# 192 instead of 160 of the 576 tokens take their experts by gathered rows, with 64 of them searched in the first tile's parts

## The reference, cut to what matters

```
q = (tb @ w_q).reshape(PEER_BLOCK, PEER_HEADS, 2, PEER_HALF)           # 8 heads, 2 x 128
s = einsum('thik,hink->thin', q, sub_keys)                             # 2 x 128 scores a head
s_top, i_top = top_k(s, 16)
cand = s_top[:, :, 0, :, None] + s_top[:, :, 1, None, :]
best_s, best_c = top_k(cand, 16)                                       # 16 experts of 16384 a head
eid = i1 * N_KEYS + i2;  g = softmax(best_s)
act = gelu(einsum('thkd,td->thk', u_tab[eid], tb))
out = einsum('thkd,thk->td', v_tab[eid], g * act)
```

## Time and profile before

| | us |
|---|---|
| median of 3 runs (lowest, highest) | 2275.99 (2273.0, 2285.11) |
| the profiled execution | 2277.83 |
| its span, first to last instruction | 2276.1 |
| PE busy | 2229.8 (98%) |
| DVE busy | 1585.5 (70%) |
| POOL busy | 1475.2 (65%) |
| ACT busy | 814.1 (36%) |

### The profile page before, as it was taken

One profiled execution on the slowest core, in us unless ns is written; L12 is line 12 of the kernel. 1 busy time (PEld: TensorE's weight loads), 2 busy tenths in 40 slices (PEclk: granted clock), 3 DMA queues, 4 the chain that ended last, 5 costly groups with the idle time before them and its releaser, 6 DMA issues.

```text
span 2276.1 us, 38281 instructions
## 1 busy us (share of the span) xinstructions
PE 2229.8 (98%) x14510; PEld 2152.9 (95%) x14510; DVE 1585.5 (70%) x2800; ACT 814.1 (36%) x1201; POOL 1475.2 (65%) x851
## 2 busy tenths in 40 slices
PE   8999999999999999999999999999989999999998
PEld 8999999997799999999999999999989999999998
DVE  7866444546678336768978889898478777777774
ACT  4443223432133002133433344444344444444442
POOL 5554333432354555557878887889778888888873
PEclk9999999999999999999999999999999999999999
DMA  6224323225763233248888897999999999999982
GB/s 215 84 80 137 97 92 101 93 96 194 250 230 128 84 126 94 84 132 275 304 286 289 291 313 248 300 331 318 355 364 396 374 369 374 385 370 375 381 311 79
DMA packets 212800, 535.19 MB, mean 235 GB/s; under 512 B 16816, under 2 KB 101168, under 8 KB 210224
## 3 DMA queue, kind: packets, MB, share of 16 engines
q1 hardware_dynamic: 111392, 234.65, 31.7%
q0 software_dynamic: 46080, 167.79, 19.7%
q10 hardware_dynamic: 55184, 130.77, 15.7%
HBM read 453.89 MB, written 79.25 MB: 234 GB/s over the span
## 4 chain that ended last, share of the span: by engine, by line
PE 85%; DVE 7%; POOL 2%; DMA 2%; ACT 1%; issue 1%; ACTq 0%; DVEq 0%; SPq 0%; POOLq 0%
PE ps L1008 47%; PE ps L732 30%; PE ps L1066 2%; POOL w_lo L706 1%; DVE prev L1875 1%; PE ps L909 1%; DMA gbuf<-gate_scratch 1%; POOL ug L698 1%; PE ps L896 1%; PE ps L904 1%; PE ps L1021 1%; PE ps L913 1%; PE ps L929 1%; DVE n_lo L1991 1%; DVE oh L2097 1%
## 5 line engine op out<-in xcount | busy, mean ns | idle before, releaser
L673 POOL TENSOR_SCALAR w_hi<-raw 128x1024 fp32r<-128x1024 f32 x129 | 139.5, 1081 | 516.3 <-issue 384.0
L706 POOL TENSOR_TENSOR w_lo<-raw,e_hi 128x1024 fp32r<-128x1024 f32 x128 | 326.4, 2550 | 95.2 <-PE ps L1008 85.3
L706 POOL TENSOR_TENSOR w_lo<-raw,w_hi 128x1024 fp32r<-128x1024 f32 x128 | 318.9, 2492 | 86.6 <-PE ps L1008 84.5
L1008 PE MATMUL ps<-p_hi,w_lo 128*128 128x416 f32 x1024 | 361.4, 353 | 0.0
L1008 PE MATMUL ps<-g_hi,w_lo 128*128 128x416 f32 x1024 | 359.6, 351 | 0.0
L675 POOL TENSOR_TENSOR w_lo<-raw,w_hi 128x1024 fp32r<-128x1024 f32 x129 | 320.7, 2486 | 10.8
L732 PE MATMUL ps<-h_hi,w_hi 128*128 128x288 f32 (+2 forms) x1216 | 273.0, 306 | 1.6 <-ACT ma L1342 1.6
L732 PE MATMUL ps<-h_lo,w_hi 128*128 128x288 f32 (+2 forms) x1216 | 262.1, 297 | 0.0
L732 PE MATMUL ps<-h_hi,w_lo 128*128 128x288 f32 (+2 forms) x1216 | 261.7, 296 | 0.0
L2075 DVE CUSTOM_DVE_ANT_0 ug<-ug,ps 128x1024 f32<-128x1024 f32 x160 | 192.3, 1213 | 72.2 <-DMA ug<-rows_u,eid 56.4
L698 POOL DMA_INDIRECT ug<-rows_u,eid x160 | 214.8, 1342 | 37.5 <-issue 24.3
(11 more groups left out here) (358 smaller groups left out, 5086.0 us busy)
## 6 DMA issues: line engine op xcount, KB each, us to landing
raw<-units SPq DMA_DIRECT2D x385, 512.0 KB
gate_scratch<-gt SPq DMA_DIRECT2D x52, 512.0 KB
activation_scratch<-ge ACTq DMA_DIRECT2D x120, 208.0 KB
abuf<-activation_scratch ACTq DMA_DIRECT2D x30, 832.0 KB
gbuf<-gate_scratch ACTq DMA_DIRECT2D x30, 832.0 KB
prev<-ssm_in ACTq DMA_DIRECT2D x8, 1024.0 KB, 6.7
ssm_s<-prev ACTq DMA_DIRECT2D x8, 1024.0 KB, 4.5
cxb<-parked_tiles ACTq DMA_DIRECT2D x8, 870.0 KB, 6.8
```

The source lines that it names most:

```text
L673: pool.tensor_scalar(w_hi[:, s, :], raw[:, r, :], 1.0, 1.0, ALU.mult, ALU.mult).then_inc(s_whi, 1)
L706: pool.tensor_tensor(w_lo[:, n % 2, :], raw[:, n % RAW, :], e_hi[m % HS_].bitcast(F32), ALU.subtract)\
L1008: last = mm(accp[par], w[:, k * P:(k + 1) * P], x_[:, k, t0:t0 + ND], start=k == 0 and i == 0, stop=k == KT - 1 and i == 2)
```

## The change

`SPREAD` goes from 4 to 2: 64 spread tokens (the columns 384 to 447), each dealt over two partitions. So 192 tokens are gathered, by 192 gathers of each table, and `ND` is 384: three whole tiles and 24 gate blocks. The half tile is gone. In its place each of the four parts of the first tile carries a third "head row" (`SLOTS` = 3): in partitions 0 to 63 one of its two heads, in 64 to 127 the other, of the 64 spread tokens. The part's scores take two PSUM banks instead of one, with four more matmuls. `column_of` finds a row's place in the tables of indices and dots.

The order is written anew: `UT` = [5, 26, 26, 26], so the search ends at unit 83 and 34 units remain beside the 24 blocks; `DOTS_T` = [0, 42, 43, 43], so all 128 dots of the last 128 tokens lie in the three searches. 24 dots of spread tokens go beside the blocks, for which their h rows are turned into PSUM once more (`h_beside`, before block 2); 8 before the last eight U units, two in each of those, two in each of the first eight V units. `M_RING` is 40 instead of 53. `scores_out(j+1)` is done at two thirds of a tile instead of half.

```diff
-SPREAD = 4
+SPREAD = 2
+SLOTS = PAIR + 1
+PART_ROWS, PART_SPREAD = PAIR * TOPK, TOPK
+PART_COLS = SLOTS * TOPK
-TT = [(T_ROWS, PH)] + [(t, PH) for t in range(0, T_HALF, P)] + [(T_HALF, PH // 2)]
-assert T_HALF % P == 0 and T_HALF <= ND
+TT = [T_ROWS] + [t for t in range(0, T_HALF, P)]
+assert T_HALF % P == 0 and T_HALF == ND
-UT = [4, 20, 20, 20, 10]
+UT = [5, 26, 26, 26]
-M_RING = M_TILE[3] + 9
+M_RING = M_TILE[2] + 9
-DOTS_T = [0, 26, 26, 26, 12]
+DOTS_T = [0, 42, 43, 43]
-DOTS_B = [(b + 1) * (N_PICK - N_SEARCH) // NB - b * (N_PICK - N_SEARCH) // NB for b in range(NB)]
-DOTS_U = [9, 0, 0, 1, 1, 1, 1, 1, 1]
-DOTS_V = [2, 2, 2, 2, 2, 2, 3, 2]
+N_BESIDE = 24
+B_SPREAD = 2
+DOTS_B = [0] * B_SPREAD + [(b + 1) * N_BESIDE // (NB - B_SPREAD) - b * N_BESIDE // (NB - B_SPREAD)
+                           for b in range(NB - B_SPREAD)]
+N_TAIL = N_PICK + N_BESIDE
+DOTS_U = [8, 2, 2, 2, 2, 2, 2, 2, 2]
+DOTS_V = [2, 2, 2, 2, 2, 2, 2, 2]
+def column_of(k):
+
+    c, a = divmod(k, PART_ROWS) if k < N_PICK else divmod(k - N_PICK, PART_SPREAD)
+    return c * PART_COLS + a + (PART_ROWS if k >= N_PICK else 0)
...
-    use += [(k, TAIL + (k - N_PICK) * 2 * GI // (N_ROW - N_PICK)) for k in range(N_PICK, N_ROW)]
+    use += [(k, TAIL + (0 if u < 0 else GI // 2 + u // 2 if u < GI else u)) for u in range(-1, 2 * GI) for k in tail_dots(u)]
...
-                for i in range(4 * c, 4 * c + 4):
-                    last = mm(ps[:, 4 + c, i % 4 * P:(i % 4 + 1) * P], q[:, i, T_ROWS:TK], key_sb[:, i, :],
+                if c >= 2:
+                    pe.wait_ge(s_scs, c - 1)
+                to = [part_scores(c)[:, r // SLOTS, r % SLOTS * NKEYS:(r % SLOTS + 1) * NKEYS] for r in range(2 * SLOTS)]
+                for i in range(2 * PAIR):
+                    qi = 2 * PAIR * c + i
+                    mm(to[i], q[:, qi, T_ROWS:TK], key_sb[:, qi, :], start=True, stop=True)
+                for i in range(2 * PAIR):
+                    qi = 2 * PAIR * c + i
+                    p0 = i // 2 * HALF
+                    last = mm(to[2 * PAIR + i % 2][p0:p0 + HALF], q[:, qi, T_HALF:T_HALF + HALF], key_sb[:, qi, :],
                               start=True, stop=True)
...
                 gates(b, b % 2, b == 0)
+                if b == B_SPREAD - 1:
+                    pe.wait_ge(s_ud, N_PICK)
+                    turn_rows(1, spread_columns, h_beside)
...
-                    if m == m0 + (n // 2 + 2 if j else n - 1) and j + 1 < len(TT):
+                    if m == m0 + (2 * n // 3 + 1 if j else n - 1) and j + 1 < len(TT):
                         scores_out(j + 1)
-                    if j and m == m0 + 3 * n // 4 + 1:
+                    if j and m == m0 + 7 * n // 8 + 1:
...
-                    act.wait_ge(s_ud, N_PICK)
+                    act.wait_ge(s_ud, N_TAIL)
...
             for c in range(PARTS):
-                search(c + 1, c * PAIR, PAIR, lambda cols: None)
+                search(c + 1, part_rows(c), SLOTS, lambda cols: None, last_of_tile=c == PARTS - 1)
...
+            dve.wait_ge(s_sc, PARTS - 1 + len(TT))
+            spread_cols = (a[:, :, ND:T_ROWS].bitcast(F32).unsqueeze(2).to_broadcast([P, KT, SPREAD, NX])
+                           for a in (g_hi, g_lo))
+            tt_(g_spread[:], *spread_cols, ALU.add).then_inc(s_gp, 1)
             one_hots(0, 0)
             for b in range(NB):
+                if b == B_SPREAD:
+                    dve.wait_ge(s_hr, 2)
                 if b + 1 < NB:
                     one_hots(b + 1, (b + 1) % 2, dots_of(b))
```

More of the change, by code:

```diff
@@ L150, in tail_dots @@
     after = DOTS_U + DOTS_V
-    d0 = N_PICK + sum(after[:u + 1])
+    d0 = N_TAIL + sum(after[:u + 1])
     return range(d0, d0 + after[u + 1])
@@ L421, in trunk, with part_scores, part_rows @@
         acc_spread = h_spread = ps[:, 6:8, :]
+        h_beside = ps[:, 2:4, :]
+        def part_scores(c):
+            return ps[:, 4 + c % 2 * 2:6 + c % 2 * 2, 0:SLOTS * NKEYS]
+        def part_rows(c):
+            return sc[:, c % 2 * PH:c % 2 * PH + 2 * SLOTS]
         turned_rows = ps[:, 2:4, :].rearrange("p a (k t) -> p (a k) t", t=P)
@@ L692, in gather @@
                 k = ROWS[j][0]
[L693 to L697, removed]
+                if k < N_PICK and k % PART_ROWS == 0:
+                    pool.wait_ge(s_eid, k // PART_ROWS + 1)
+                table, k = (rows_u, column_of(k)) if k < N_ROW else (rows_v, column_of(k - N_ROW))
                 pool.indirect_dma_start(
@@ L1015, in scores @@
             def scores(j):
-                t0, heads = TT[j]
+                t0 = TT[j]
                 for i in range(2 * PH):
[L1018 to L1022, removed]
+                    last = mm(ps[:, 4 + i // 4, i % 4 * P:(i % 4 + 1) * P], q[:, i, t0:t0 + P], key_sb[:, i, :],
+                              start=True, stop=True)
                 last.then_inc(s_sc, 1)
@@ L1035, in picks @@
                 pe.wait_ge(s_pk, j + 1)
-                parts = [slice(0, P)] if TT[j][1] == PH else [slice(0, HALF), slice(HALF, P)]
                 for i in range(3):
-                    for p_ in parts:
-                        n = p_.stop - p_.start
-                        to = (1, 0, 2)[i] * P
-                        last = mm(S0[p_, to:to + n], pick[p_, i, 0:n], ident[p_, p_], start=True, stop=True)
+                    to = (1, 0, 2)[i] * P
+                    last = mm(S0[:, to:to + P], pick[:, i, :], ident[:], start=True, stop=True)
                 last.then_inc(s_pkT, 1)
@@ L2074, in row_dot @@
                 rows = row_landed(k)
-                dve.tensor_tensor_reduce(rows, rows, h_rows if k < N_PICK else h_spread, 1.0, 0.0, ALU.mult, ALU.add, dots[:, k:k + 1])\
+                dve.tensor_tensor_reduce(rows, rows, h_rows if k < N_PICK else h_beside if k < N_TAIL else h_spread,
+                                         1.0, 0.0, ALU.mult, ALU.add, dots[:, column_of(k):column_of(k) + 1])\
                     .then_inc(s_ud, 1)
@@ L2179, in _ @@
             dve.wait_ge(s_eid, PARTS)
-            for j, (t0, heads) in enumerate(TT[1:], 1):
-                np_ = heads * TOPK
+            for j in range(1, len(TT)):
                 due = [*range(sum(DOTS_T[:j]), sum(DOTS_T[:j + 1]))]
@@ L2186, in step @@
                 def step(cols):
-                    passed[0] += cols * 8 // heads
+                    passed[0] += cols
                     if due and passed[0] * (DOTS_T[j] + 1) >= SEARCH * (DOTS_T[j] - len(due) + 1):
                         row_dot(due.pop(0))
-                search(PARTS + j, 0, heads, step, j - 1)
+                search(PARTS + j, sc, PH, step, j - 1)
                 dve.sem_inc(s_pk, 1)
-                if heads < PH:
-                    for i in range(SPREAD):
-                        to = slice(i * NX, (i + 1) * NX)
-                        own0, pick_0 = i * NX // HALF * HALF + HALF - NX, i * NX % HALF
-                        own, here = slice(own0, own0 + NX), slice(pick_0, pick_0 + N_ROW - N_PICK)
-                        dve.tensor_copy(pick0[to, N_PICK:], pick[own, 2, here])
-                        last = stt(coef[to, N_PICK:], pick[own, 0, here], float(NKEYS), pick[own, 1, here],
-                                   ALU.mult, ALU.add)
-                    link(last)
-                    dve.tensor_copy(eid[:, N_PICK:], coef[:, N_PICK:]).then_inc(s_eid, 1)
-                    spread_cols = (a[:, :, ND:T_ROWS].bitcast(F32).unsqueeze(2).to_broadcast([P, KT, SPREAD, NX])
-                                   for a in (g_hi, g_lo))
-                    tt_(g_spread[:], *spread_cols, ALU.add).then_inc(s_gp, 1)
                 for k in due:
```

64 lines of the change are left out of this document (31 added, 33 removed).

## The result

The changed kernel took 2288.46 us (2283.61 to 2291.87, 13 runs) against 2278.99 us for the kernel before on the same chip: a ratio of 1.0039, 95% interval 1.0028 to 1.005. The forecast was 2244, with a range of 2212 to 2278 and a chance of 0.14 for a result within 0.5% of no change, which this is. So the forecast of a gain was wrong, in sign too.

The account below looks back on a forecast made before the run. PE, working 98% of the span, was taken as the bound, with POOL and DMA close behind. From 2277.8 us the stage terms 3.6 + 16.7 - 51.1 + 4 - 7.6 + 0.5 = -33.9 gave 2244 us, range 2212 to 2278.

Parts of the forecast that it names:

- Columns: Expert matmuls on PE: 32 fewer columns save 13.6 ns each; 384 columns start every 175 ns; 84 to 87 us possible.
- Queries: Up to 1002.7 us: four more small matmuls a part on PE, +0.9 us a part, +3.6 in all.
- Searches: 1002.7 to 1375.7 us: 85 units instead of 76, three tiles bound by PE or POOL; +16.7 us.
- The other two become POOL's: Search tiles two and three: POOL, not PE, sets the time, 119.2 and 1.5 us, then 118.0 us.
- these waits should mostly vanish in its slack: Searches: DVE's 39.5 us of waits for landed rows mostly go, its work being 107 of 119 us.
- a sign of being wrong: Searches: the prediction is wrong if DVE's waits for landed rows pass 20 us a tile.
- Gate blocks: 1375.7 to 1623.8 us: 24 blocks and 34 units, PE and DVE in lockstep with 8 idle, 197 us; -51.1 us.
- Between: Units 119 to 143, between U and V units: POOL's cycles sum to 123, 130 us taken; +4 us, bounds 118 and 140.
- V units: Unit 144 to the end: POOL 4.44 and DMA 4.52 us a unit, 4.50 taken; -7.6 us.
- the first (DMA gives only 374): Rival for the V units: DMA already full at 374 GB/s, 4.86 us a unit, 2289 us in all; chance 0.12.
- The second, lockstep: Rival: PE, POOL and DVE, nearly equal, add +10 in searches, +11 in blocks, +6 between the stages: 2271 us; chance 0.15.
- The third, PE alone: Rival: PE stays the bound, late gathers absorbed, DMA reaching 410 GB/s: 2207 us; chance 0.1.

Follow-up runs that it names:

- e2: Changed kernel with POOL computing only half the width of each w_lo of the expert units: 2247.82 us, ratio 0.9852.
- e5: Changed kernel with a row's slot reused four units after the row is due instead of three (ROW_LAG 4): 2279.89 us, ratio 1.0002.
- e6: Changed kernel with a row's slot reused two units after the row is due instead of three (ROW_LAG 2): 2306.52 us, ratio 1.0111.
- e10: Kernel before the change with a row's slot reused four units after the row is due instead of three (ROW_LAG 4): 2281.91 us, ratio 1.0024.
- e9: Changed kernel with the gate stores tied to weight loads 5, 5, 6 and 6 units behind the pair instead of 6, 6, 7 and 8: 2271.98 us.
- e8: Changed kernel with the gathers between U and V units issued evenly, three a unit from 123 to 130, instead of in bursts: 2285.1 us, ratio 1.0029.
- e3: Changed kernel loading only half of each V weight unit after the first few: 2276.64 us, ratio 0.998.
- e4: Changed kernel with both half of each w_lo and, in the V units, half of each weight load: 2208.68 us, ratio 0.9678.
- e11: Changed kernel with slots reused after four units, even gathers between U and V units, and earlier gate stores: 2264.04 us, ratio 0.9939.
- e1: Kernel before the change with expert matmuls over 384 of 416 columns, gathers and all else kept: 2231.36 us, ratio 0.978.

## Why the prediction was wrong

Point by point, by its own terms.

*Columns*: right, 176.0 ns at 384 columns.

*Queries, +3.6 forecast, +7.9 measured.* A part's added score matmuls take 0.59 us, where 0.9 was forecast. 4.9 of the 7.9 lie before 900 us, in code that the change doesn't touch; over all kernels here that point comes anywhere from 893 to 900 us, at 894.9 in the profile of before and at 899.8 in that of after. From there to the first expert matmul it is 107.5 us in every profile without the change and 110.2 to 110.8 in every one with it. So the change itself costs 3.2 us, near the forecast.

*Searches, +16.7 forecast, +40.0 measured: the step that failed.* "The other two become POOL's" was right (e2). Wrong was to take the larger of PE's and POOL's work as the stage, with almost nothing for their waits on each other and on DVE. The three tiles took 122.5, 126.1 and 122.3 us from w_lo to w_lo, where 115.3, 120.7 and 118.0 were forecast. The first missed most. It was "PE's", by 112.8 us against POOL's 112.1 (107.5 and 4.6); measured are 6.4 us in which PE waits for w_lo, 8.6 in which POOL waits for PE, and 2.8 in which POOL waits for dots. Two engines this close don't give the larger of two sums. In the second, POOL's instructions sum to 64.0 (26 w_lo) and 45.4 (44 gathers), with 7.3 between issues and 1.2 in shorter gaps: 117.9, when 119.2 was forecast for work with the bf16 hold. What was missing is waiting: 4.0 us for dots, which I had put at nothing, and 4.2 us for PE, where I had 1.5. An engine whose work was to fill the whole stage leaves nothing to absorb either. The sentence "these waits should mostly vanish in its slack" looked at DVE's mean (107 of 119 us) and not at the 15 us at the end of a search in which hardly a dot is done. They did not vanish but grew, from 39.5 us to 55.7: 18.1, 20.6 and 17.0 by tile, the second over the 20 that the prediction had named as a sign of being wrong. That the waits for dots are a part of it shows in e5 and e6 (-9, +17 us in the searches for a unit more or less), and e10 shows that it was not there before. 6.4 of the 23.3 missed lie at the two ends; of those, 4.7 behind the last search go with e5.

*Gate blocks, -51.1 forecast, -39.5 measured: the second step that failed.* PE, DVE and POOL were counted; the way out of the gates was not. The stores are placed by units, and the change shortened a pair of blocks from 3.31 to 2.83 units without moving them. I had asked what each moved step issues, but not what becomes too late when steps only come closer together. With it mended (e9) the stage is 194.7 us, where 197 had been forecast, so the count of the three engines was good.

The prediction set the lockout between DVE and POOL aside, since taken to the letter it gave 267 us for this stage. That sum was made wrongly: its 6.5 us of one-hots a block are means in which DVE's own waiting for POOL is already counted. Alone a one-hot takes 2.28 us and a w_lo 2.4. POOL and DVE of e9 beside each other:

```profile
1501.37 2.41 POOL L725 TENSOR_TENSOR w_lo<-raw,e_hi 128x1024 fp32r<-128x1024 f32 x1
...
1506.80 2.40 POOL L725 TENSOR_TENSOR w_lo<-raw,e_hi 128x1024 fp32r<-128x1024 f32 x1
```

```profile
1502.22 3.72 DVE L2119 TENSOR_TENSOR oh<-iota,keyb 128x4096 f16<-128x4096 f16 x1 [4.24 <-PE ps L1087]
...
1507.00 4.35 DVE L2123 TENSOR_TENSOR oh<-oh,partb 128x4096 f16<-128x4096 f16 x1
1511.28 2.28 DVE L2119 TENSOR_TENSOR oh<-iota,keyb 128x4096 f16<-128x4096 f16 x1
```

Each one-hot that starts during a w_lo ends about 2.2 us after that w_lo. In all 44 such overlaps in the gate blocks of the kernel after, the two need at least 4.49 us from the first start to the last end. By the lockout that the Trainium skill states (SBUF — State Buffer, "SBUF: two separate sides") whichever starts first has the port for its whole instruction, and the trace agrees. Summed with the lengths alone, 24 blocks of two one-hots and 34 w_lo are 24 x 4.56 + 34 x 2.4 = 191 us, an estimate from these rows, so the 194.7 measured do not speak against the rule. It also means that DVE and POOL together had as little room here as PE with its 189.

*Between, +4 forecast, +10.4 measured.* The right cause, a size too small: the eight gathers behind one unit part two w_lo by 12.3 us, PE stalls and the granted clock is 0.92. Both 136.4 and the 127.4 with the gathers spread evenly (e8) lie inside the bounds of 118 and 140.

*V units, -7.6 forecast, -7.7 measured*: right, 4.487 us a unit for 4.50, by DMA's 405 GB/s with POOL 1% behind (e2, e3, e4). That it is right to 0.1 us is luck: from w_lo of unit 144 on, e5 to e9 and e11, with the same V units, take 521 to 524 us against 518.5 here.

*The rivals.* Of the first (DMA gives only 374) nothing came: it gave 405 over 400 us. The some 358 GB/s between HBM and SBUF of the Trainium skill (DMA: Bandwidth & Descriptors, "Where 436 GB/s comes from") do not bind here: the same row, of a kernel on one core, is above them. The second, lockstep, priced the searches at +10 and the blocks at +11 over the forecast, which is the right direction and half the size in the searches (+23.3); in the blocks the size is right (+11.6) but the reason was the stores. The third, PE alone, did not come. None of the rivals had the stores, and none had the clock: each term took PE at 2.4 GHz, though its rate was half for 3.6 us after a stall of 5.11 us, and the mean granted clock 0.97 in searches and blocks.

Open is why the V units take back what e8's edit gives between the stages, by a third in e8 and wholly in e11, and why only 3.4 us of e8 show in the medians.

## What to carry to other kernels

Work taken from a full engine is worth only what the next one leaves: measure that by cutting the work alone (e1: 48 of 84 us), then price the added work on the engine that becomes the bound (1.07 us a gather here), before the two are joined. At that engine add its waits to its work; slack elsewhere doesn't cover them, and two engines with nearly equal sums take longer than either. When a stage gets shorter, go through everything that is placed by its steps, stores and buffer reuse above all: one line that had not been moved along cost 16 of the 24 us by which the mended order beats the changed one. And before adding up two engines that hold each other up, take their lengths alone, not means in which the holding is already counted.

## What the runs showed of the hardware

A long stall of PE cost more than its length. After 5.11 us idle eleven matmuls started 320 ns apart, then 175, so the granted clock was at the 1.2 GHz level for 3.6 us and 1.6 us were lost on top (11 x 145 ns). By the Trainium skill (TensorE: Matmul & The Clock Gate, "Wait — 56ns, not 53.3ns?") starts are columns over the clock apart while the clock is low: 384 / 1.2 = 320, and the trace agrees. At full clock it gives columns / 2.4 and 2.5 ns, 162.5; the rows show 176.0 with a weight load for each matmul. A gate block coming out of a stall took 3.57 us instead of 1.85. In e9 the blocks' mean clock rose from 0.97 to 1.00 as the stalls went.

DMA held 405 GB/s for 400 us on one core, with shares of 1.03, when weights, gathered rows and reloaded tiles came together; relieving POOL did not raise it (e2).

A w_lo on POOL and a one-hot on DVE do not run at once: 2.4 and 2.28 us alone, at least 4.49 us together in all 44 overlaps of the kernel after. Beside the search's wide bf16 operation of 4.42 us even the issue of a gather took 4.42 us instead of 0.96.
